# Recurrence and mixer of a two-block model: block copies moved from VectorE to ScalarE, the mixer's first split and second weight piece moved into the recurrence

## What is computed

```
def chunk_scan(q, k, v, logf, s0):
    """S_t = diag(f_t) S_{t-1} + k_t v_t^T, o_t = S_t^T q_t, chunkwise. q,k,logf (B,L,H,K); v (B,L,H,V); s0 (B,H,K,V)."""
...
def hgrn_readout(o, g, norm_g):
    bn, L = o.shape[:2]
    o = rmsnorm(o, norm_g).reshape(bn, L, HG_WIDTH)
    return (o * jax.nn.silu(g.astype(jnp.float32))).astype(g.dtype)
...
        mix = jnp.concatenate([rmsnorm(y_hy, hy_norm_g[l]).astype(x.dtype), y_hg.astype(x.dtype)], axis=-1) @ w_out[l]
        x = x + g1 * mix
```

## Time and profile before

| | us |
|---|---|
| median of 3 runs | 3856.48 (3848.94 to 3859.07) |
| the profiled execution | 3860.58 |
| its span, first to last instruction | 3858.6 |
| TensorE busy | 3548.3 (92%) |
| VectorE busy | 2580.7 (67%) |
| ScalarE busy | 1876.5 (49%) |
| recurrence, in the trace | about 811 to 1006.2 |
| mixer, in the trace | about 1006.9 to 1145 |

### The profile page before, as it was taken

How to read it: one execution, slowest core, us unless ns; L and a number is a source line. 1 busy time by engine, 2 the same in 40 slices (tenths; PEclk the granted TensorE clock), 3 DMA queues, 4 the chain that set the end, 5 groups by cost and what they waited for, 6 DMA issues and landing times. The chain is left out here.

```text
span 3858.6 us, 43103 instructions
## 1 busy us (share of the span) xinstructions
PE 3548.3 (92%) x16760; PEld 2831.9 (73%) x16760; DVE 2580.7 (67%) x2881; ACT 1876.5 (49%) x2427; POOL 781.0 (20%) x624
## 2 busy tenths in 40 slices
PE   7999989976788999999999998999898989999989
PEld 4887744676676778888788786788776677887857
DVE  6546266879668888888888886565675645416753
ACT  5211111366545777777777776341564233515731
POOL 2100024600120101101102104200343233103422
PEclk9999989978888999999999999999999999999999
DMA  5554314220438999999999995365411542624133
GB/s 201 198 181 155 114 58 163 96 104 33 148 122 312 360 373 379 368 386 373 377 371 371 371 363 164 115 206 175 158 55 57 179 129 83 178 108 170 48 109 115
DMA packets 322788, 774.50 MB, mean 201 GB/s; under 512 B 26072, under 2 KB 110419, under 8 KB 322328
## 3 DMA queue, kind: packets, MB, share of 16 engines
q1 hardware_dynamic: 299802, 694.94, 49.6%
q0 software_dynamic: 17856, 66.33, 5.3%
q10 hardware_dynamic: 4928, 10.49, 0.8%
HBM read 660.21 MB, written 111.48 MB: 200 GB/s over the span
## 5 line engine op out<-in xcount | busy, mean ns | idle before, releaser
L3398 DVE TENSOR_TENSOR first_expert_w_low<-shared_z,first_expert_w_high 128x2048 fp32r<-128x2048 f32 x127 | 299.0, 2395 | 82.3 <-ACT first_expert_w_high L3351 82.0
L3398 DVE TENSOR_TENSOR moe_w_low<-moe_w_raw,moe_w_high 128x2048 fp32r<-128x2048 f32 x128 | 287.2, 2284 | 48.7 <-ACT moe_w_high L3351 48.5
L3398 DVE TENSOR_TENSOR moe_w_low<-shared_z,moe_w_high 128x2048 fp32r<-128x2048 f32 x128 | 287.0, 2282 | 24.5 <-ACT moe_w_high L3351 24.5
L3351 ACT ACTIVATE first_expert_w_high<-shared_z 128x2048 fp32r<-128x2048 f32 x126 | 234.9, 1918 | 116.1 <-DMA shared_z<-in_exp_w 116.1
L3351 ACT ACTIVATE moe_w_high<-moe_w_raw 128x2048 fp32r<-128x2048 f32 x128 | 238.3, 1910 | 94.2 <-DMA moe_w_raw<-in_exp_w 86.4
L3626 POOL TENSOR_SCALAR layer_att_p<-layer_att_p,layer_att_rinv,layer_att_neg_lam 128x1280 f32<-128x1280 f32 (+1 forms) x72 | 173.2, 2405 | 530.0 <-DVE layer_att_neg_lam L3655 315.3
L3351 ACT ACTIVATE moe_w_high<-shared_z 128x2048 fp32r<-128x2048 f32 x128 | 238.5, 1914 | 59.6 <-DMA shared_z<-in_exp_w 58.5
L177 PE MATMUL moe_bank<-moe_w_high,first_expert_xgT_high 128*128 128x512 f32 x640 | 252.5, 394 | 0.7 <-DVE moe_w_low L3398 0.7
L3633 DVE TENSOR_REDUCE layer_att_nb<-layer_att_scores 128x1 f32<-128x1280 f32 (+1 forms) x144 | 194.8, 1368 | 85.7 <-PE layer_att_scores L3538 84.9
L179 PE MATMUL moe_bank<-moe_w_high,first_expert_xgT_low 128*128 128x512 f32 x640 | 250.6, 392 | 0.0
L178 PE MATMUL moe_bank<-moe_w_low,first_expert_xgT_high 128*128 128x512 f32 x640 | 250.6, 392 | 0.0
(11 more groups left out here) (660 smaller groups left out, 9484.0 us busy)
## 6 DMA issues: line engine op xcount, KB each, us to landing
shared_z<-in_exp_w SPq DMA_DIRECT2D x128, 2048.0 KB, 10.0
moe_w_raw<-in_exp_w SPq DMA_DIRECT2D x64, 2048.0 KB, 10.1
shared_z<-in_w_in SPq DMA_DIRECT2D x48, 512.0 KB, 6.5
first_raw<-in_w_in SPq DMA_DIRECT2D x32, 512.0 KB, 7.4
front_vec<-in_ada_w POOLq DMA_DIRECT2D x16, 1024.0 KB, 6.0
proj_t<-front_out SPq DMA_DIRECT2D x48, 256.0 KB, 2.0
shared_z<-in_w_mod SPq DMA_DIRECT2D x24, 512.0 KB, 4.5
k_high<-layer_front_staged SPq DMA_DIRECT2D x20, 512.0 KB
```

What stands on the lines that cost most here:

```text
L3351: nc.scalar.activation(hi, x, ACT.Copy).then_inc(high, 1)
L3398: nc.vector.tensor_tensor(lo, x, hi.bitcast(F32), ALU.subtract).then_inc(low, 1)
```

## The change

1. In `outer` and `inner`, step j = 0 uses access patterns without their last dimension of size 1.
2. WIDE = 2, FINE = 5: levels 0 to 4 keep VectorE's `select`. Levels 5 and 6 are done by ScalarE's new `block_copy`, which copies only the blocks that belong to the level: 4 blocks of 32 partitions by 4x32 for level 5, 2 of 64 by 4x64 for level 6, for each half. TensorE's waits on the masked semaphore for these levels become waits on the new semaphore blocked.
3. The split of the mixer's first weight piece goes into the recurrence: the high part on ScalarE after level 4 of the last head (`early_weights`), the low part on VectorE after the last carry. The split of the first filter rows goes there too: ScalarE after the last kt copy (`early_rows`), GpSimd behind it.
4. The second weight piece is loaded on SP in the recurrence, after a wait for all output products of heads 0 to 2 (its room is in use until then), ahead of the load of out_g. The mixer's loads lose it, and the fourth piece has a place of its own and no wait.
5. `first_squares` is cut in two: heads 0 to 2 ahead of the last but one output copy, head 3 after it.
6. In the mixer TensorE runs the first 12 products of the first tile ahead of the transposes of that tile.

Core of the diff:

```diff
@@ -2332,6 +2344,9 @@
                                      ).then_inc(core.out_early, 16)
                     for half in range(2 if h >= 2 else 0):
                         store_o(2 * (h - 2) + half)
+                sp.wait_ge(odone, PAIRS * (H - 1))
+                sp.dma_start(core.out_raw, io["w_out"][0][BANK:2 * BANK, 0:BANK].rearrange("(k p) n -> p k n", p=P)
+                             ).then_inc(core.out_piece, 16)
                 sp.dma_start(out_g, core.vg[0:P, BANK:2 * BANK]).then_inc(core.load[2].sem, 16)
@@ -2384,6 +2402,19 @@
+                def block_copy(h, half, j):
+
+                    act.wait_ge(prod, 2 * (LEVELS * h + j) + half + 1)
+                    act.wait_ge(diagonal, 2 * h + half + 1)
+                    act.wait_ge(masked, 2 * FINE * (h + 1) - 1 + half)
+                    width = 1 << j
+                    score = ring(16 * h + 2 + 2 * j + half)[:, :].rearrange("p (t c) -> p t c", c=P)
+                    for k0 in range(0, P, width):
+                        q0 = k0 ^ width
+                        last = nc.scalar.activation(unit(h, half)[k0:k0 + width, :, q0:q0 + width],
+                                                    score[k0:k0 + width, :, q0:q0 + width], ACT.Copy)
+                    last.then_inc(blocked, 1)
@@ -2401,14 +2432,20 @@
-                def first_squares():
-
-                    junk = kt[0][:, 0, :]
-                    act.wait_ge(ds, H * NSB)
-                    act.wait_ge(ocopied, 2 * H - 1)
-                    for h in range(H):
-                        core.act(act, nc.scalar.activation(junk, out_o[:, h, :], ACT.Square, accum_out=ss0[:, h:h + 1]))
-                    core.act(act, nc.scalar.activation(rms0, ss0, ACT.Sqrt, bias=core.eps[:, 0:1], scale=1.0 / P))
+                def first_squares(heads):
+
+                    act.wait_ge(ocopied, 2 * heads[-1] + 1)
+                    for h in heads:
+                        core.act(act, nc.scalar.activation(q_[1][:, 0:P], out_o[:, h, :], ACT.Square, accum_out=ss0[:, h:h + 1]))
+
+                def early_weights():
+                    act.wait_ge(core.out_early, 32)
+                    act.wait_ge(odone, PAIRS * (H - 2))
+                    nc.scalar.activation(core.out_split[0], core.out_w[:, :, :], ACT.Copy).then_inc(w_high, 1)
+
+                def early_rows():
+                    act.wait_ge(odone, PAIRS * (H - 1))
+                    nc.scalar.activation(core.out_y[0], core.out_hyena, ACT.Copy).then_inc(y_high, 1)
@@ -2435,13 +2472,21 @@
+                        if not more and j == 4:
+                            early_weights()
+                        if j >= FINE:
+                            for half in range(2):
+                                block_copy(h, half, j)
                 first_gate()
                 for k in range(NSB):
                     kt_copy(H - 1, k)
                     if k in (1, 2):
                         o_copy(2 * (H - 2) + k - 1)
+                early_rows()
+                first_squares(range(H - 1))
                 o_copy(2 * H - 2)
-                first_squares()
+                first_squares(range(H - 1, H))
+                core.act(act, nc.scalar.activation(rms0, ss0, ACT.Sqrt, bias=core.eps[:, 0:1], scale=1.0 / P))
                 o_copy(2 * H - 1)
@@ -2575,20 +2625,21 @@
-                    ends = [[3 * half, 2], [1, half]]
+                    ends, spread = ([[3, 2]], []) if j == 0 else ([[3 * half, 2], [1, half]], [[0, half]])
@@ -2638,10 +2689,13 @@
-                        for half in range(2):
+                        for half in range(2 if j < FINE else 0):
                             select(h, half, j)
                 for k in range(NSB):
                     carry_state(H - 1, k)
+                dve.wait_ge(w_high, 1)
+                core.dve(dve, nc.vector.tensor_tensor(core.out_split[1], core.out_w[:, :, :], core.out_split[0].bitcast(F32),
+                                                      ALU.subtract))
@@ -2698,8 +2755,6 @@
                     half, part = divmod(p, 2)
-                    if p == 3:
-                        sp.wait_ge(w_low, 2)
@@ -2825,23 +2883,23 @@
-                turn(0)
                 for t in range(NT):
...
                             if n == 0 and k == 4:
-                                pe.wait_ge(y_low, 2)
+                                turn(0)
+                                pe.wait_ge(y_low, 1)
```

More of the change, by code:

```diff
@@ L2237, in stage_hgrn @@
     PAIRS, RING = NT // 2, 4
+    WIDE = 2
+    FINE = LEVELS - WIDE
+    with Stage(core, name + "_out") as out_st:
+        out_st.sb("gap", [P, 36352])
+        split_high = out_st.sb("split_high", [P, 4, BANK], F32R)
+        core.out_raw = out_st.sb("raw", [P, 4, BANK])[:, :, :]
+        core.out_y = tuple(out_st.sb(k, [P, 4, P], F32R)[:, :, :] for k in ("y_high", "y_low"))
+        core.out_split = split_high[:, :, :], out_st.sb("split_low", [P, 4, BANK], F32R)[:, :, :]
     with Stage(core, name) as st:
```

103 lines of the change are left out of this document (58 added, 45 removed).

## The result

The changed kernel took 3866.65 us (median of 8 runs, 3864.12 to 3873.7), the kernel before in the same session 3857.78 us (8 runs). The ratio is 1.0029, with an interval of 1.0017 to 1.0041: slower by 11 us, between 6.6 and 15.8. The profiled execution was the slowest of the eight, 3873.7 us with a span of 3871.9 us; the profiled one of before had a span of 3858.6.

A forecast was written before the change was run, and what follows sets the result against it. VectorE was taken to bound the heads (45.37 of 46 us), a dependent chain the tail, ScalarE the mixer's opening. Gains 7.6, losses 9.7, net 2.1 us longer: 3858.6 us against the runs' median 3856.48; range 3850 to 3867.

The forecast's parts named there:

- The DMA that moved: Recurrence's tail: gate tile's load behind SP's wait and the weight piece delays the first kt copy; loss 7.7 us, bounds 5.0-8.2.
- Rival A: Recurrence's tail: gate tile isn't late or the tail has slack; 7.6 us shorter, 3848.9 us; chance 0.11.
- TensorE's clock: Tail: TensorE idles some 7 us in the wait and its clock falls to 1.2 GHz; loss 2.0 us.
- Rival C: Tail: TensorE falls to 1.2 GHz and never recovers there; 9.4 us in place of 2.0, 3866.0 us; chance 0.10.
- Blocks by ScalarE: Recurrence's four heads: selections of levels 5 and 6 leave VectorE, copies 0.16 us apart; gain 2.6 us.
- Rival B: Recurrence's heads: copies cost like the far row, place(6) always late; loses 2.0 instead of gaining 2.6, 3863.2 us; chance 0.13.
- Squares ahead: Tail: three of four squares move into ScalarE's idle time ahead of its last chain; gain 1.3 us.
- Mixer: Mixer's opening: first result 23.1 us after the start instead of 26.85; gain 3.7 us, between 3.0 and 4.5.
- The eight tiles: Mixer after its first result: eight tiles follow at a steady pace that the change leaves alone; no term in the sum.
- Moves that should be hidden: Last head and tail: weight split and filter rows' split moved into the recurrence fall into slack; price 0.
- First step's patterns: Step j = 0 of the recurrence: instructions have the same sizes before and after; price 0.
- Rivals D and E: Recurrence: all selections count without waits, 3840.8 us, chance 0.03; new patterns bring step 0 to full rate, 3850.5, chance 0.02.

The follow-up runs named there:

- e1: Changed kernel with the gate tile's load put back ahead of SP's wait for head 2's output products: 3856.61 us, ratio 0.9991.
- e2: Kernel before with SP waiting for head 2's output products ahead of the gate tile's load, no weight piece there: 3862.64 us, ratio 1.0018.
- e7: e1 with all levels selected by VectorE (WIDE = 0), no block copies: 3857.73 us, ratio 1.0001.
- e3: Changed kernel with all levels selected by VectorE (WIDE = 0), gate tile still late: 3866.99 us, ratio 1.0032.
- e10: e9 with the mixer's last weight piece issued ahead of the loads of tile 2: 3852.71 us, ratio 0.9986.
- e4: Changed kernel with ScalarE's block copies for level 6 alone (WIDE = 1), gate tile still late: 3864.23 us, ratio 1.0017.
- e11: e10 with 14 extra unread transposes on TensorE ahead of the last head's output products: 3852.72 us, ratio 0.9990.
- e8: Kernel before with the mixer's split weights' rows 320 bytes lower within 2048 bytes, no instruction added or moved: 3856.2 us, ratio 0.9991.
- e12: Changed kernel with gate tile first, all selections on VectorE, split weights 320 bytes higher, last weight piece earlier: 3850.85 us, ratio 0.9984.
- e9: Changed kernel with gate tile first, block copies for level 6 alone, split weights placed 320 bytes higher: 3852.36 us, ratio 0.9990.
- e5: Changed kernel with 60 extra unread transposes on TensorE in the wait for the late gate tile: 3864.53 us, ratio 1.0009.

## Why the prediction was wrong

I had 3858.6 us and no change that can be measured; it became 3866.65, near the upper end of the range and clearly slower. The prediction failed in the size of its terms. The mechanism that I called the deciding term was right, and so was the sign of my sum; its size was wrong, 2.1 us net where the traces have 8.4.

- **The DMA that moved: right.** Expected 7.7 us, measured 7.2 (0.69 to 7.88). The gate tile's landing lay between its own bounds, as ScalarE's row at 990.32 shows: 5.7 us after the weight piece's issue at the latest, where I took 6.3. e1 and e2 show it from both sides. Rival A falls.
- **TensorE's clock: mechanism right, term mis-sized.** 2.0 taken, 3.3 measured. The fall behind the wait was expected from the earlier trace rows; the second one, in the output products at 1004 to 1007, was not, and the last output products are the stretch where TensorE's pace counts in full. Rival C has about the measured time, 3866.0, but not for its reason: the clock came back twice, and cost 3.3, not 9.4.
- **Blocks by ScalarE: the step that failed most, by 2.4 us: the spacing of the copies, and the worth of a pair of selections.** I took 0.16 us from the plain 128-column copy and its follower; the eight copies of level 5 last 2.22 us, one alone 0.27, so they start (2.22 - 0.27) / 7 = 0.28 apart, beyond the 0.25 that I had named as a sign of being wrong. Head 0 lost 1.8 instead of 1.0, head 1 gained 1.8 instead of 2.5, head 2 0.4 instead of 1.1 (1.2 by my own rows, since 938.31 - 937.1 is 1.2), head 3 lost 0.2 instead of nothing. Together they gained 0.2 where I had 2.6. The spacing explains head 0 (2.22 us of copies, not 1.4, ahead of place(6)) and fits head 2, where VectorE waited 0.57 us for place(6). Head 1 had no such wait; there the price of a pair was too high. A pair of selections had also covered VectorE's wait for its own result, so one pair gone gave 1.1 us at the head's start and 0.9 at level 6, not 1.24 each, and 0.2 went to a later wait. Rival B had the copies 0.41 us apart and 2.0 us lost in the body; both came out between its figures and mine. The Trainium skill ("ScalarE: Activation LUTs", Rules for kernel authors) budgets 0.3 us per ACTIVATE with a bias pointer and 0.83 ns per element, as an estimate 3.3 us for the run of eight. Measured were 2.22, and I had taken 1.4: the rule that I set aside pointed the right way, and was too high by 1.1 where I was too low by 0.8.
- **Block copies and the clock: a step that I did not take.** That the block copies also cost 1.6 us of clock at the tail's end once the gate tile is early (e1 against e7) I had nowhere; in the changed kernel, with it late, they cost 0.2 there (e3).
- **Squares ahead: right.** 1.3 expected, 1.35 measured.
- **Mixer: mis-sized.** 3.7 expected, 2.4 measured. I had let the heads' tile and the last piece be there in time; ScalarE waited 2.29 and 2.04 us for them, as long as before in sum. The queue's order behind the first megabyte had not changed, and the stage had only become shorter ahead of it. e10 shows how: the wait passes to the transfer that is next.
- **The eight tiles: a step that I did not take.** I wrote that the steady pace is one "that the change leaves alone". The instructions are the same, but the operands lie elsewhere, and each product of 512 columns took 0.006 us more: 2.0 us.
- **Moves that should be hidden: right.** e7 has the early splits and the weight piece, without a late gate tile and without block copies, and its tail takes 11.77 us against 11.72.
- **First step's patterns:** no effect, as expected: VectorE's outer product of step 0 takes 2.54 to 2.57 us, its two inner products 2.61 to 2.63, in both kernels. Rivals D and E did not happen.

So what my sum lacked is 2.4 (body), 1.3 (clock), 1.3 (mixer) and 2.0 (placement), less 0.5 for the gate tile and 0.1 for the squares: 6.3 us from unrounded terms, the difference between 8.4 and 2.1. Each is small, but all except the last two went one way: for the copies, for the selections and for the mixer's transfers I had taken the favourable case.

What stays open: why the clock falls a second time in after and in e3, but not in e2 and e4; and why it falls in the last output products when ScalarE writes blocks and the gate tile is early, although TensorE is exactly as busy in the 12 us ahead of the idle time as in e7 (4.00 of 4 us, then 7.05 of 8). Before that its clock had come back later: 0.52 in e1 and 0.66 in e7 over the 5 us that end 4 us ahead of the turns. That fillers cure it (e11) says only that idle time takes part. Open is e8's whole time too.

## What to carry to other kernels

A load whose consumer stands ahead of a chain must be issued before any wait that is put on the same queue, and the cost of being late is the wait plus what TensorE's clock loses in it. Where a change moves tensors, compare the spacing of unchanged instructions at the same granted clock: here a layout cost 2.0 us where the rewritten opening of the mixer saved 2.4. A rewrite with several small gains should be taken apart: here the order of two loads brought back 10 us, and with three smaller edits besides (selections on VectorE, the gap sizes, an earlier load; e12) the loss became a gain of 6.

## What the runs showed of the hardware

- Products of 512 fp32r columns follow one another at 0.2267 us or at 0.2333 us, at a granted clock of 1.00, by where the rows of the streamed operand start: 320 bytes of shift within 2048 bytes, with the other operand in place, switch between the two, in both directions (e8, e9). Whether the place itself counts or its relation to the other operand's was not told apart.
- Eight ScalarE copies of 32 partitions x 128 elements out of PSUM, at changing partition offsets, ran 0.28 us apart (after); a 128 x 128 copy let a larger one start 0.16 us behind it.
- A 256 KB load issued 0.42 us behind a 1 MB load on the same queue landed 5.2 us after its own issue (after), and 2.8 us after it where nothing was ahead (e2).
- After 7.5 us without work TensorE's granted clock was 0.50 (1.2 GHz) from 992.9 to 996.5 in after; it was 1.00 from 998 to 1002 and 0.52 again from 1003.7 to 1007. Sixty transposes that nobody reads, 6.7 us of them in the wait, left it at 1.00 in every stretch from 987.6 to 1010.8 (e5).
